# Query rows loaded ahead of value pages, and rope ahead of key products on GpSimd, in a hybrid decoder step

## What is computed

```python
h = rmsnorm(x) ; z = h @ w_in                       # q, k, v of two groups of heads, 512 columns each
q1, q2, ka = rope(z[...]) ; qf, kf, vf, logf = ...  # rope for the differential heads only
oa = (softmax(q1 k1^T) - lam * softmax(q2 k2^T)) v  # prompt, causal, 4 heads
of = softmax(qf kf^T + C[t] - C[s]) vf              # prompt, causal, 8 heads, C = cumsum(logf)
# the samples: the same two attentions of one query row over the 8 cached pages (gathered by
# page_table from cache_diff_k, cache_fox_k, cache_diff_v, cache_fox_v, cache_fox_logf) and the new row
x = x + rmsnorm(merge(oa, of) @ w_o)
x = x + rmsnorm(conv_ffn(x))                        # w_gate, w_up, depthwise conv, gelu, w_down
```

## Time and profile before

| | us |
|---|---|
| median of 3 runs | 1514.48 |
| lowest, highest | 1509.99, 1522.22 |
| the profiled execution | 1509.19 |
| its span | 1507.4 |
| TensorE busy in the span | 1431.7 (95%) |
| VectorE, ScalarE, GpSimd busy | 855.6, 637.0, 365.6 |
| granted TensorE clock, mean | 0.989 |

### The profile page before, as it was taken

One profiled execution on the slowest core, in us unless ns is written; L12 is line 12 of the kernel. 1 busy time (PEld: TensorE's weight loads), 2 busy tenths in 40 slices (PEclk: granted clock), 3 DMA queues, 4 the chain that ended last, 5 costly groups with the idle time before them and its releaser, 6 DMA issues. The chain is left out here.

```text
span 1507.4 us, 26822 instructions
## 1 busy us (share of the span) xinstructions
PE 1431.7 (95%) x10396; PEld 1290.3 (86%) x10396; DVE 855.6 (57%) x1378; ACT 637.0 (42%) x1194; POOL 365.6 (24%) x548
## 2 busy tenths in 40 slices
PE   7999989999989889879999999999999999999998
PEld 6999776777767667558789999999999999999998
DVE  6412567566554445544547876666777645444663
ACT  6723655444354434543323533323333324443543
POOL 5213876764645352021100000000000000000120
PEclk9999999999999999999999999999999999999999
DMA  5213556677755644622223222222222236655773
GB/s 183 57 34 90 178 164 210 201 231 221 237 187 178 191 158 127 220 86 71 79 82 100 70 75 69 85 85 85 75 81 78 63 140 202 201 186 185 235 259 111
DMA packets 174842, 209.93 MB, mean 139 GB/s; under 512 B 22052, under 2 KB 118892, under 8 KB 174677
## 3 DMA queue, kind: packets, MB, share of 16 engines
q1 hardware_dynamic: 174714, 208.21, 43.4%
HBM read 178.37 MB, written 29.88 MB: 138 GB/s over the span
## 5 line engine op out<-in xcount | busy, mean ns | idle before, releaser
L600 POOL TENSOR_TENSOR k_page<-k_page,q_bc 128x256 f32<-128x256 f32 x256 | 187.2, 763 | 132.2 <-DMA k_page<-in_cache_fox_k 100.3
L1197 PE MATMUL PS<-ht_hi,w_hi 128*128 128x344 f32 x576 | 195.9, 340 | 5.9 <-ACT z_raw L724 2.5
L1197 PE MATMUL PS<-ht_hi,w_lo 128*128 128x344 f32 x576 | 186.4, 324 | 0.0
L1197 PE MATMUL PS<-ht_lo,w_hi 128*128 128x344 f32 x576 | 186.3, 323 | 0.0
L2415 PE MATMUL PS<-act_hi,wd_hi 128*128 128x344 f32 x528 | 169.0, 320 | 2.6 <-DVE act_lo L2253 2.6
L2415 PE MATMUL PS<-act_hi,wd_lo 128*128 128x344 f32 x528 | 168.6, 319 | 0.0
L2415 PE MATMUL PS<-act_lo,wd_hi 128*128 128x344 f32 x528 | 168.4, 319 | 0.0
L2250 DVE TENSOR_TENSOR wd_lo<-wd_raw,wd_hi 128x1024 fp32r<-128x1024 f32 (+1 forms) x88 | 87.8, 1002 | 115.6 <-ACT act_hi L2064 95.5
L832 ACT ACTIVATE probs<-probs,stat 128x256 f32<-128x256 f32 (+7 forms) x128 | 98.8, 773 | 127.3 <-DVE stat L1076 126.7
L1197 PEld LDWEIGHTS PS<-ht_hi,w_hi 128*128 128x128 f32 x576 | 110.4, 192 | 31.6 <-issue 23.9
L2061 ACT ACTIVATE wd_hi<-wd_raw 128x1024 fp32r<-128x1024 f32 (+1 forms) x88 | 74.2, 845 | 140.8 <-DMA act_raw<-a_dram 104.9
(11 more groups left out here) (280 smaller groups left out, 3283.9 us busy)
## 6 DMA issues: line engine op xcount, KB each, us to landing
wd_raw<-in_w_down SPq DMA_DIRECT2D x44, 512.0 KB, 3.5
k_page<-in_cache_diff_k SPq DMA_DIRECT2D x64, 256.0 KB, 2.8
k_page<-in_cache_fox_k SPq DMA_DIRECT2D x64, 256.0 KB, 3.1
v_page<-in_cache_diff_v SPq DMA_DIRECT2D x64, 256.0 KB, 2.8
v_page<-in_cache_fox_v SPq DMA_DIRECT2D x64, 256.0 KB, 3.0
w_raw<-in_w_in SPq DMA_DIRECT2D x24, 512.0 KB, 4.7
a_dram<-conv SPq DMA_DIRECT2D x22, 516.0 KB, 3.1
act_raw<-a_dram SPq DMA_DIRECT2D x66, 172.0 KB, 3.6
```

Of the source, the lines that this page charges most:

```text
L600: ins = pool.tensor_tensor(kpage[:, g % 2, c:c + PIECE], kpage[:, g % 2, c:c + PIECE], qbc[:, c:c + PIECE], ALU.mult)
L1197: ins = pe.matmul(PS[0:rows, z_bank(c), 0:THIRD], b[:, k, :], a[:, k, third(i)], start=(k == 0 and p == 0), stop=(k == KC - 1 and p == 2))
```

## The change

Two edits. On SyncE the load of the query row of sample b leaves `load_key_page` for those samples for which page 8b - 3 is multiplied at least two jobs before page 8b - 1. That holds for samples 1 to 5 and not for 6 and 7. It is then issued in the job in which page 8b - 1 is multiplied (jobs 3, 10, 17, 24, 31), with the same wait, but ahead of that job's value page, gates, weights and key page. On GpSimd the rope of a chunk goes ahead of the key products of its job.

```diff
+            query_first = lambda b: k_job(PAGES * b - 3) + 1 < k_job(PAGES * b - 1)
+
+            def load_query(b):
+                sp.wait_ge(mult_done, PAGES * b)
+                sp.dma_start(qbc[:, :], io["qs_dram"][b:b + 1, :].to_broadcast([P, 2 * GRP])).then_inc(qbc_in, 16)
+
             def load_key_page(g):
...
-                if b and n == 0:
-                    sp.wait_ge(mult_done, g)
-                    sp.dma_start(qbc[:, :], io["qs_dram"][b:b + 1, :].to_broadcast([P, 2 * GRP])).then_inc(qbc_in, 16)
+                if b and n == 0 and not query_first(b):
+                    load_query(b)
...
+                for b in range(1, DB):
+                    if k_job(PAGES * b - 1) == J and query_first(b):
+                        load_query(b)
                 for g in range(DB * PAGES):
                     if (v_job(g - 2) if g >= 2 else v_job(0) - 2) == J:
                         load_value_page(g)
...
+                if J:
+                    for c, h in fill(J - 1)[0] + fill(J - 1)[1]:
+                        if h:
+                            rope(c)
                 for g in k_pages(J):
                     if g % PAGES == PAGES - 1:
                         later_pages(g // PAGES)
                     multiply(g)
-                if J:
-                    for c, h in fill(J - 1)[0] + fill(J - 1)[1]:
-                        if h:
-                            rope(c)
```

## The result

| | before | changed |
|---|---|---|
| median of 18 runs | 1515.37 us (1509.99 to 1522.22) | 1522.67 us (1517.31 to 1529.62) |
| ratio to before | | 1.005, 95% interval 1.0035 to 1.0065 |
| span of the profiled execution | 1507.4 us | 1516.1 us |
| mean granted clock | 0.989 | 0.989 |

The change costs 7.6 us (5.3 to 9.9), half a percent: a small loss that is measured, and inside the range of the forecast (1520.5, 1508 to 1530).

A forecast was written before the change was run, and what follows sets the result against it. TensorE was taken as the bound, busy 439.07 of 480 us (91%) in attention. Unit 0's +3.0, 0 in jobs 8 to 30 and job 33's +3.0 made +6.0 us: 1520.5 us against 1514.5, range 1508 to 1530.

The forecast's parts named there:

- Mechanism: SyncE's queue: query loads wait for the last product, so going first gains 0.0 to 0.4 us and holds back later loads.
- All signs named for it: Idle before matmuls at 172 gone; VectorE waits about 3 us for page 8; job 33: ScalarE waits 4 us, TensorE 3.
- the bound of 0.4 us: Query loads in SyncE's queue: going ahead can make them sooner by at most 0.0 to 0.4 us.
- Rope first: GpSimd's rope ahead of key products: wins TensorE 2.48 us in job 2, but products come 2.8 us later.
- Gone by job 5: The rope's 2.48 us gain is lost by job 5, where VectorE's maxima stand 0.6 us later than before.
- Unit 0: Sample 1's query load delays key page 8; TensorE ends unit 0 3.0 us later, rope's gain included; bounds 2.0 and 4.0.
- the landing of key page 8: In unit 0, key page 8 is issued at 187.2 and lands 3.1 us later, at 190.3.
- Samples 2 to 4: Jobs 10, 17, 24: cost nothing, since VectorE reaches the first page late, with margins of 1.3 to 2.6 us.
- Job 33: Weights held behind sample 5's query load land 4.7 us after issue; TensorE idles 3.0 us more; bounds 2.1 to 6.4.
- The 3.2 us: Landing time of job 33's 512 KB weights by the skill page, making that stall 1.5 us; the prediction kept its row.
- The clock, rival B: Clock falls behind new stalls, 3.5 us each: 1527.5 us if behind both, 1524 if behind one; chance 0.18.
- Sum: Whole kernel: +3.0 in unit 0, 0 in jobs 8 to 30, +3.0 in job 33: +6.0 us, from +4.1 to +10.4.

## Why the prediction was right, point by point

**Mechanism.** Right: the query loads start on the end of the products (184.69 for 184.65, 397.28 for 397.25), so going first in the queue makes them no sooner and holds back what stands behind. All signs named for it are there. VectorE waits 4.66 us for page 8 (3 forecast), ScalarE 5.85 us for weights (4), TensorE 4.23 us in job 33 (3), and the idle time in front of the matmuls at 172 is gone. One reading was off: the four places of the earlier trace rows are samples 1, 4, 5 and 6, and sample 6's load is not moved. Those of samples 2 and 3 were issued 0.4 and 0.2 us behind the last product, so the bound of 0.4 us on what could be won stands.

**Rope first.** "Gone by job 5" holds: alone it is worth 0 within 3 us. The end of page 7 was forecast at about 184.0 and came at 184.65.

**Unit 0.** Forecast +3.0, measured +3.9 (1.4 to 6.7) with rope and load together. The term that was too small is the landing of key page 8: issued at 187.43, near the 187.2 of the sum, it landed 4.6 us later, not 3.1, so its products began at 192.20 and not at 190.3. The sum put this cost under the query row. The table shows that it belongs to the pair: 2.2 us of idle time of TensorE that neither edit brings alone, and about 2 us of clock, which was costed at nothing. What takes up the delay of a single edit is not shown. It is not a reserve of VectorE's that the trace of before would show: there VectorE took page 8 at 189.78, right on the end of its products at 189.74.

**Samples 2 to 4.** Forecast 0, measured 0 within 3.5 us.

**Job 33.** Forecast +3.0; alone it measured +5.9 (2.9 to 9.1), and taking it out of the changed kernel gave 3 back. The runs agree on the place, and leave its size between 3 and 6; by the table it is 5.4, the difference between the means of the two groups. Two terms were small: the landing (6.2 us, not 4.7, still under the 8.2 of the earlier trace rows; this very load had taken 5.3 before), and the clock, costed at nothing. The latter stood at 0.85, 0.50 and 0.79 in the three windows from 406 to 412. The 3.2 us that the prediction worked out from the Trainium skill, page "DMA: Bandwidth & Descriptors", section "Anatomy of one DMA", is further off still. That fit is given there for transfers issued by GpSimd, and these are issued by SyncE.

**The clock, rival B.** Its condition came true in the profile: the clock fell behind both new stalls. But the time is not the 1527.5 us that it gave. What was wrong in it is that it took the falls of before as fixed and added new ones. In 140 to 700 us I summed (1 - clock) over windows of 2 us: 10.2 us for before, 13.7 for the changed kernel. Before had falls at 286 to 292 and 450 to 458 which the changed kernel has not, or has shorter. The profiles of the kernels that measured 0 have sums of 13.6 to 22.2. So the net is 3.4 us in this pair, and the scatter between executions is larger than that. The table shows the same size where it can be laid to the stalls: against the means of the groups without them, 2.0 us more are lost in unit 0 and 1.5 in jobs 32 to 40.

**Sum.** The parts measured one by one, 3.9 for the pair in unit 0, 0, and 5.9 for sample 5, make 9.8 against 7.6 together, in agreement within intervals of 2.5 to 3 us each. The forecast's 6.0 was 1.6 us short. Its closeness is in part luck: TensorE's new idle time is 2.2 and 3.9 us by the table, 6.1 together for the 6.0 forecast, but forecast as 3.0 and 3.0, and some 3.5 us of clock come on top.

## What to carry to other kernels

In this queue, which issues in order, a load that waits for a semaphore is a gate: moving it ahead paid only where its wait was already met at that place, and with whatever is used with it; otherwise it delays every load behind it, and the one that was wanted soonest after its landing (here weights for two jobs later) set the price. Look at the issue time against the release time of each such load: where they coincide nothing is to be won, and where they are 5 us apart, as for sample 7, there was. Two edits that each cost nothing measurable can cost together when they delay the same instruction, so they have to be measured together as well. And profiles of kernels that are alike in a stretch, laid side by side, settle what medians with 3 us of uncertainty and one pair of profiles can't.

## What the hardware did that I had not expected

Three loads that mattered landed later than their medians, each with other loads issued close to it. That the neighbours are the cause was not tested. The weights took 6.2 us when issued behind query rows and a pair of value pages and ahead of key page, value page and gates (median 5.1, smallest 3.9 in the changed kernel); the key page of 256 KB took 4.6 us behind the weights (median 3.2); sample 7's query rows took 5.9 us behind the key page (kernel before, median 4.4).

The granted clock does not fall by one rule that these rows would give. It stayed at 1.00 after the 2.48 us of idle time at 172 in the kernel before, and fell to 0.61 and 0.50 in the windows from 172 in the kernel with sample 1's load alone, with 2.67 us of idle time up to 173.09 and the same instructions around it. Most falls of these stages come behind a stall, yet not behind the same stall in every profile. It has to be read from each execution, and a difference of 3 us between two profiles may be that alone. The scatter of the times is largely the clock's: of 116 runs of the kernel before, the 25 with a mean clock of 0.989 or more took 1507.2 to 1515.5 us, the 23 with 0.983 or less 1516.8 to 1523.5.
